# Four sums of weight blocks per combined pair: by adding transfers of GpSimd's queue instead of by VectorE

## The chip, the core and the metric

The kernel runs on one core of one Trainium2 chip. The metric is device time in microseconds (us), the median of several runs; less is better. "ACT" is ScalarE, "DVE" VectorE, "PE" TensorE, "POOL" GpSimd and "SP" SyncE.

## What is computed

One step of a two-layer encoder trunk with 512 prompt rows and 8 x 16 sample rows, 640 rows in all, and a model width of 1024. Each layer does this (the reference, cut to what matters here):

```python
h = x @ w_in            # differential-attention q/k/v | window q/k/v | two branch gates
A = differential attention (8 heads);  B = sliding-window attention (16 heads, sinks)
x = LayerNorm(ALPHA * x + (sigmoid(g_a) * (A @ w_branch_a) + sigmoid(g_b) * (B @ w_branch_b)) @ w_o)
x = LayerNorm(ALPHA * x + relu(x @ w_up) ** 2 @ w_down)
```

All products are fp32-accurate: each operand is split into a high part (fp32r) and the remainder, and each product is three matmuls: high x high, high x low, low x high.

## The kernel before

**Tiling.** Weights stream from DRAM in chunks of 128 x 1024 fp32 (512 KB) through four slots of the tile `w_raw`. SP issues the load of a chunk (L489) once the chunk four places earlier has been split. For each chunk ACT makes the high part by a copy and DVE the low part by a subtraction. Activations are kept transposed, 640 rows in two halves of 320.

**Combined pairs.** Part of the feature tiles are not multiplied one by one. Two tiles (two chunks of weights) form a pair, and each pair's 2 x 2 blocks of weights, a11 and a12 in the first chunk and a21 and a22 in the second, are multiplied with the 2 x 2 blocks of the activations by a scheme with seven block products in place of eight. There are five groups of four pairs in each layer: eight gate tiles (part 0), the branch product of A (`BRANCH`), and parts 1, 2 and 3 of `w_up`. That is 40 pairs in the program. Each block product is 4 x 3 matmuls of 128 x 320, on TensorE in the order o = 0 to 6 (`combined_pair` of the tensor block, L575 to L577).

The stationary operands of the seven products are o=0: a11, o=1: S1 = a21 + a22, o=2: S2 = S1 - a11, o=3: a12, o=4: S3 = a11 - a21, o=5: S4 = a12 - S2, o=6: a22. The four sums are made by DVE in `weight_sums` (L2400, L2403, L2407, L2411). S1 goes to the tile `s_one`; the others overwrite blocks of `w_raw`: S3 takes a21's place, S2 takes a11's, S4 takes a12's. So S2 waits until a11 has been split (`part_ready` 5q+1) and S4 until a12 has been (5q+4); q numbers the pairs through the program.

**Splitting.** For each operand ACT copies the high part (`part_highs`, L1571) and DVE subtracts (`part_low`, L2420). There is one buffer for each o, so the high part for the next pair is made after this pair's product o.

**Seeds.** Three times in each pair ACT copies a partial result from one PSUM bank to another (`up_seed`, L1600): seed 0 after product 0, needed by product 2; seed 1 after product 2, needed by product 4; seed 2 after product 4, needed by product 6. Each engine executes its own instructions in written order. In a pair of `w_up` (parts 1 to 3), ACT's order from one seed to the next is, for pair u:

```python
up_square(u-1, even); up_relu(u-1, odd, half 0); part_highs(u, (6,)); up_seed(u, 0)
up_square_high(u-1, odd); part_highs(u+1, (0,)); up_square(u-1, odd); up_fifth(u)
part_highs(u+1, (1,)); up_seed(u, 1); part_highs(u+1, (2,)); up_relu(u, even, half 0)
part_highs(u+1, (3,)); up_seed(u, 2); up_relu(u, odd, half 1); part_highs(u+1, (4, 5))
up_relu(u, even, half 1); up_square_high(u, even)
```

The gate group and the branch group have the same order without the squares (`gate_pair`, `branch_pair`). DVE, during pair u, makes the lows of the squares of pair u-1 (L2444), the lows of operands 0 to 3 of pair u+1 between the sums, and `up_add` (L2439), which adds `p5` to a bank.

Between the groups stand ordinary row products (`w_down`, L642 to L644) and the attention heads. The first pair of a group is prepared while they run.

Of the kernel before, what the change touches and what calls it, by code (L numbers as in the profile page):

```python
# [26 lines left out]
D = 1024  # L27
# [73 lines left out]
def build(nc, x_rows, x_cols, k_cache, v_cache, swa_kc, swa_vc, swa_k_keep, swa_v_keep, weights, cols,  # L101
# [3 lines left out]
    with ctx:  # L105
# [188 lines left out]
        def up_bank(x):  # L294
            return PS[:, x, 0:HALF]
# [30 lines left out]
        dec_recip, dec_r_ready = sem("dec_recip"), sem("dec_r_ready")  # L326
# [9 lines left out]
        unit_recip, unit_r_ready = sem("unit_recip"), sem("unit_r_ready")  # L336
        unit_second, unit_probs = sem("unit_second"), sem("unit_probs")
# [27 lines left out]
        s_summed, part_hi_made, part_ready = sem("s_summed"), sem("part_hi_made"), sem("part_ready")  # L365
# [120 lines left out]
        def _(sp):  # L486
# [43 lines left out]
            sp.wait_ge(keep_stored, 32)  # L530

# [584 lines left out]
        def _(act):  # L1116
# [426 lines left out]
            def part_highs(l, part, u, products):  # L1543
# [29 lines left out]
            def up_seed(l, part, u, i):  # L1573
# [26 lines left out]
                fn(up_bank(dst), up_bank(src), ACT.Copy).then_inc(seeded, 1)  # L1600
# [174 lines left out]
            for l in range(DEPTH):  # L1775
# [72 lines left out]
                for part in range(FF_PARTS):  # L1848
# [9 lines left out]
                    else:  # L1858
                        q, n = pair_at(l, part, FF_PAIRS - 1)
                        act.wait_ge(part_ready, 5 * (q + 1))  # L1860
                        act.wait_ge(s_summed, 4 * (q + 1))
# [11 lines left out]
        def _(dve):  # L1873
# [86 lines left out]
            def unit_combine(l, h, i):  # L1960
# [59 lines left out]
            def head(l, h, p, first, more, uses):  # L2020
# [18 lines left out]
                v.reciprocal(d_r, d_l).then_inc(dec_recip, 1)  # L2039
                dve.wait_ge(dec_recip, n + 1)  # L2040
                v.tensor_scalar(d_r, d_r, lam_row[:, bass.ds(l, 1)], None, ALU.mult).then_inc(dec_r_ready, 1)
                dve.wait_ge(dec_r_ready, n + 1)
# [47 lines left out]
            def a_sum(l, t):  # L2090
# [14 lines left out]
                elif t == 3:  # L2105
# [3 lines left out]
                    v.tensor_tensor(ta_full[3][:], b22, b12, ALU.subtract).then_inc(t_ready, 1)  # L2109
# [20 lines left out]
            def branch_pair(l, u):  # L2130

                last = u == FF_PAIRS - 1
                if not last:
                    weight_sums(l, BRANCH, u + 1, 1)
                    weight_sums(l, BRANCH, u + 1, 3)
                else:
                    part_low(l, BRANCH, u, 4)
# [5 lines left out]
                else:  # L2143
                    part_low(l, BRANCH, u + 1, 0)
                    weight_sums(l, BRANCH, u + 1, 2)
# [3 lines left out]
                if not last:  # L2149
                    weight_sums(l, BRANCH, u + 1, 4)  # L2150
# [192 lines left out]
            def x_sums(l, which, u):  # L2343
# [20 lines left out]
                elif u == 2:  # L2364
# [4 lines left out]
                    v.tensor_tensor(full[3], b22, b12, ALU.subtract).then_inc(t_ready, 1)  # L2369
# [17 lines left out]

            def weight_sums(l, part, u, which):

                q, n = pair_at(l, part, u)  # L2390
                first, second = raw[:, raw_of(0, n)[0], :], raw[:, raw_of(1, n)[0], :]
                a11, a12, a21, a22 = first[:, 0:BANK], first[:, BANK:D], second[:, 0:BANK], second[:, BANK:D]
                if which == 1:
                    for s in range(2):
                        j, loads = raw_of(s, n)
                        dve.wait_ge(raw_loaded[j], 16 * loads)
                    if q:
                        dve.wait_ge(s_summed, 4 * q - 1)
                        dve.wait_ge(part_ready, 5 * q - 3)
# [436 lines left out]
```

## Time and profile before

| | |
|---|---|
| median of 3 runs | 2199.17 us (2198.41 to 2199.62) |
| the profiled execution's own time | 2201.14 us |
| its span, first to last instruction | 2199.4 us |
| PE busy | 2179.4 us, 99% |
| DVE busy | 1408.5 us, 64% |
| ACT busy | 1135.4 us, 52% |
| POOL busy | 0.2 us |
| mean granted TensorE clock | 0.998 |
| read from and written to HBM | 236.35 and 25.95 MB |

The shares are averages over the whole span. "Idle before" in a row is the time in which the engine stood still ahead of an instruction, and the arrow names what ended it. "Us to landing" of a DMA is the time from the issuing instruction to the semaphore that says that the data has landed.

### The profile page before, as it was taken

The page shows a single profiled execution, that of the slowest core. Times are in us where ns is not written, and L with a number is a line of the kernel's source. Part 1 is how long each engine was busy: PE and PEld are TensorE (multiplying, and loading weights), DVE is VectorE, ACT ScalarE, POOL GpSimd, SP SyncE. Part 2 cuts the span into 40 slices and gives each one's busy share as a digit, 9 for nine tenths or more (in the row PEclk, how much of TensorE's full clock was granted, in tenths as well). Part 3 has the DMA queues.
Part 4 walks back from the last instruction along what each step waited for, and adds up shares of the span by engine and source line. Part 5 has one row for each costly group of instructions (what it writes and reads, how often), then busy time and mean ns, then how long its engine had stood idle before and what let it go on. Part 6 is the DMA issues. An engine that isn't in the chain of part 4 may idle for free.

```text
span 2199.4 us, 38374 instructions
## 1 busy us (share of the span) xinstructions
PE 2179.4 (99%) x15286; PEld 1985.0 (90%) x15290; DVE 1408.5 (64%) x2324; ACT 1135.4 (52%) x2401; POOL 0.2 (0%) x4
## 2 busy tenths in 40 slices
PE   9999999999999999999999999999999999999998
PEld 8988888999989898989889888889999898989897
DVE  6757777766556563736667577776764665736466
ACT  4457766586423353626234676766863232626261
POOL 0000000000000000000000000000000000000000
PEclk9999999999999999999999999999999999999999
DMA  5366562431431222222333765524214312222231
GB/s 185 101 245 247 204 223 84 139 111 59 139 125 39 78 78 85 87 77 87 105 108 105 276 229 193 200 82 144 100 49 149 115 49 77 87 77 87 67 108 75
DMA packets 68160, 268.18 MB, mean 122 GB/s; under 512 B 10984, under 2 KB 12648, under 8 KB 61296
## 3 DMA queue, kind: packets, MB, share of 16 engines
q1 hardware_dynamic: 43136, 152.75, 20.6%
q10 hardware_dynamic: 24848, 112.99, 14.6%
q8 instruction: 122, 2.00, 0.4%
q14 instruction: 54, 0.44, 0.1%
HBM read 236.35 MB, written 25.95 MB: 119 GB/s over the span
## 4 chain that ended last, share of the span: by engine, by line
PE 97%; DVE 2%; issue 1%; ACT 1%; DMA 0%; ACTq 0%; DVEq 0%
PE PS L549 10%; PE PS L643 10%; PE PS L644 10%; PE PS L642 10%; PE PS L551 10%; PE PS L550 10%; PE PS L575 8%; PE PS L576 8%; PE PS L577 8%; PE PS L768 2%; PE PS L793 2%; PE PS L732 1%; PE PS L683 1%; PE PS L898 1%; PE PS L782 1%; PE PS L879 1%
## 5 line engine op out<-in xcount | busy, mean ns | idle before, releaser
L549 PE MATMUL PS<-xt_hi,w_hi 128*128 128x320 f32 x1312 | 421.1, 321 | 4.7 <-ACT rope_c L1271 3.6
L551 PE MATMUL PS<-xt_hi,w_lo 128*128 128x320 f32 x1312 | 405.3, 309 | 0.0
L550 PE MATMUL PS<-xt_lo,w_hi 128*128 128x320 f32 x1312 | 405.1, 309 | 0.0
L1127 ACT ACTIVATE w_hi<-w_raw 128x1024 fp32r<-128x1024 f32 x194 | 203.6, 1058 | 362.4 <-PE PS L644 285.9
L1914 DVE TENSOR_TENSOR w_lo<-w_raw,w_hi 128x1024 fp32r<-128x1024 f32 x194 | 235.4, 1222 | 236.9 <-ACT w_hi L1127 233.3
L642 PE MATMUL PS<-w_hi,act_a_hi 128*128 128x512 f32 x800 | 312.1, 390 | 0.0
L643 PE MATMUL PS<-w_lo,act_a_hi 128*128 128x512 f32 x800 | 311.4, 389 | 0.0
L644 PE MATMUL PS<-w_hi,act_a_lo 128*128 128x512 f32 x800 | 311.4, 389 | 0.0
L549 PEld LDWEIGHTS PS<-xt_hi,w_hi 128*128 128x128 f32 x1312 | 246.6, 188 | 16.3 <-issue 10.1
L550 PEld LDWEIGHTS PS<-xt_lo,w_hi 128*128 128x128 f32 x1312 | 246.9, 188 | 0.1
L551 PEld LDWEIGHTS PS<-xt_hi,w_lo 128*128 128x128 f32 x1312 | 246.3, 188 | 0.0
L644 PEld LDWEIGHTS PS<-w_hi,act_a_lo 128*128 128x128 f32 x800 | 150.2, 188 | 31.3
L642 PEld LDWEIGHTS PS<-w_hi,act_a_hi 128*128 128x128 f32 x800 | 150.2, 188 | 31.0 <-issue 0.5
L643 PEld LDWEIGHTS PS<-w_lo,act_a_hi 128*128 128x128 f32 x800 | 150.2, 188 | 30.5
L1154 ACT ACTIVATE rope_s<-PS 32x320 f32<-32x320 f32 x352 | 150.6, 428 | 50.9 <-DVE z_all L1905 23.2
L2420 DVE TENSOR_TENSOR part_lo<-w_raw,part_hi 128x512 fp32r<-128x512 f32 x130 | 88.7, 689 | 60.7 <-ACT part_hi L1571 58.5
L1571 ACT ACTIVATE part_hi<-w_raw 128x512 fp32r<-128x512 f32 x130 | 80.1, 623 | 33.6 <-DVE w_raw L2407 32.5
L1571 ACT ACTIVATE w_hi<-w_raw 128x512 fp32r<-128x512 f32 x110 | 66.5, 623 | 59.5 <-PE PS L644 48.5
L576 PE MATMUL PS<-t_lo,part_hi 128*128 128x320 f32 x288 | 89.0, 309 | 0.0
L577 PE MATMUL PS<-t_hi,part_lo 128*128 128x320 f32 x288 | 89.0, 309 | 0.0
L575 PE MATMUL PS<-t_hi,part_hi 128*128 128x320 f32 x288 | 89.0, 309 | 0.0
L2257 DVE SCALAR_TENSOR_TENSOR rows<-rows,PS 128x512 f32<-128x512 f32 x100 | 67.2, 685 | 33.9 <-PE PS L644 33.9
(282 smaller groups left out, 4581.3 us busy)
## 6 DMA issues: line engine op xcount, KB each, us to landing
w_raw<-in_weights SPq DMA_DIRECT2D x274, 512.0 KB, 3.5
kc<-in_k_cache ACTq DMA_DIRECT2D x32, 1024.0 KB, 7.7
vc<-in_v_cache ACTq DMA_DIRECT2D x16, 2048.0 KB, 8.8
gates_kept<-a_t ACTq DMA_DIRECT2D x8, 640.0 KB, 6.6
k_out<-k_t ACTq DMA_DIRECT2D x16, 320.0 KB, 2.4
v_out<-rows ACTq DMA_DIRECT2D x2, 2560.0 KB, 17.3
mix_a<-a_t ACTq DMA_DIRECT2D x2, 2560.0 KB, 13.2
rope_c<-gates_kept ACTq DMA_DIRECT2D x10, 320.0 KB, 3.5
```

The lines of the kernel that those rows point to most:

```text
L549: mm(out, wh, hi[:, k, c], start=(k == 0), stop=False)
L550: mm(out, wh, lo[:, k, c], start=False, stop=False)
L551: last = mm(out, wl, hi[:, k, c], start=False, stop=(k == KT - 1))
L575: mm(up_bank(x), wh, moving[0][:, k], start=first and k == 0, stop=False, skip_group_check=True)
L576: mm(up_bank(x), wh, moving[1][:, k], start=False, stop=False, skip_group_check=True)
L577: last = mm(up_bank(x), wl, moving[0][:, k], start=False, stop=(k == KH - 1), skip_group_check=True)
L642: mm(out, xh, wh, start=(k == 0), stop=False)
L643: mm(out, xh, wl, start=False, stop=False)
L644: last = mm(out, xl, wh, start=False, stop=(k == KT - 1))
L1127: fn(w_hi[slot][:], raw[:, j, :], ACT.Copy).then_inc(w_hi_made[s], 1)
L1154: last = fn(rope_s[dst:dst + 32, half * HALF:(half + 1) * HALF], PS[src:src + 32, bank_of(0, half), 0:HALF], ACT.Copy, scale=scale)
L1914: v.tensor_tensor(w_lo[slot][:], raw[:, raw_of(s, n)[0], :], w_hi[slot][:].bitcast(F32), ALU.subtract)\
```

## The change

`weight_sums` and its four calls for each pair are gone. GpSimd, which had no work, gets a program of its own: for each of the 40 pairs five DMAs of 128 x 512 fp32 (256 KB) on its queue, four of which add to what lies at the destination (`accum_op=ALU.add`). All four sums are sums now: S1 = a21 + a22, S2 = a11 + S1, S3 = a11 + a21, S4 = a12 + S2. In order to get the same result, three places take the opposite sign: the third sum of the activations (`b12 - b22`), the first two seeds (scale -1), and the even tile's `up_add` (a subtraction). Two of the operands of the additions are read from DRAM again, where `w_raw` has been overwritten. ACT's waits on `s_summed` become waits on the transfers' semaphores. Some semaphores of the attention part are merged, with the same waits.

```diff
+        @block.gpsimd
+        def _(pool):
+            def pair_sums(l, part, u):
+
+                q, n = pair_at(l, part, u)
+                first, second = raw[:, raw_of(0, n)[0], :], raw[:, raw_of(1, n)[0], :]
+                j, loads = raw_of(1, n)
+                pool.wait_ge(raw_loaded[j], 16 * loads)
+                pool.dma_start(second[:, 0:BANK], weights[2 * n, :, 0:BANK], accum_op=ALU.add)\
+                    .then_inc(s_three_added, 16)
+                if q:
+                    pool.wait_ge(part_ready, 5 * q - 3)
+                if u == 0 and part == 0:
+                    if l == 0:
+                        pool.wait_ge(masks_ready, 2)
+                        pool.wait_ge(lam_link, 6)
+                    else:
+                        pool.wait_ge(input_rows, l * ROW_STEPS)
+                elif u == 0 and part == BRANCH:
+                    pool.wait_ge(unit_pv, 3 * HEADS * (l + 1))
+                elif u == 0 and part == 1:
+                    pool.wait_ge(ln_rows, ROW_STEPS * (l + 1))
+                pool.dma_start(s_one[:], weights[2 * n + 1, :, 0:BANK]).then_inc(s_one_loaded, 16)
+                pool.wait_ge(s_one_loaded, 32 * q + 16)
+                pool.dma_start(s_one[:], weights[2 * n + 1, :, BANK:D], accum_op=ALU.add).then_inc(s_one_loaded, 16)
+                pool.wait_ge(s_one_loaded, 32 * (q + 1))
+                pool.wait_ge(part_ready, 5 * q + 1)
+                pool.dma_start(first[:, 0:BANK], s_one[:], accum_op=ALU.add).then_inc(s_two_added, 16)
+                pool.wait_ge(s_two_added, 16 * (q + 1))
+                pool.wait_ge(part_ready, 5 * q + 4)
+                pool.dma_start(first[:, BANK:D], first[:, 0:BANK], accum_op=ALU.add).then_inc(s_four_added, 16)
...
@@ part_highs @@
-                        act.wait_ge(s_summed, 4 * q + {1: 1, 4: 2, 2: 3, 5: 4}[o])
+                        if o == 1:
+                            act.wait_ge(s_one_loaded, 32 * (q + 1))
+                        elif o == 2:
+                            act.wait_ge(s_two_added, 16 * (q + 1))
+                        elif o == 4:
+                            act.wait_ge(s_three_added, 16 * (q + 1))
+                        else:
+                            act.wait_ge(s_four_added, 16 * (q + 1))
...
@@ up_seed @@
-                fn(up_bank(dst), up_bank(src), ACT.Copy).then_inc(seeded, 1)
+                fn(up_bank(dst), up_bank(src), ACT.Copy, scale=1.0 if i == 2 else -1.0).then_inc(seeded, 1)
...
@@ the third sum of the activations (also for A) @@
-                    v.tensor_tensor(full[3], b22, b12, ALU.subtract).then_inc(t_ready, 1)
+                    v.tensor_tensor(full[3], b12, b22, ALU.subtract).then_inc(t_ready, 1)
...
@@ weight_sums and all its calls @@
-                    v.tensor_tensor(s_one[:], a21, a22, ALU.add).then_inc(s_summed, 1)
-                    v.tensor_tensor(a21, a11, a21, ALU.subtract).then_inc(s_summed, 1)
-                    v.tensor_tensor(a11, s_one[:], a11, ALU.subtract).then_inc(s_summed, 1)
-                    v.tensor_tensor(a12, a12, a11, ALU.subtract).then_inc(s_summed, 1)
...
@@ up_add @@
-                v.tensor_tensor(pair_tile(part, u, odd)[:, HALF:ROWS], up_bank(X2 if odd else X3), p5[:], ALU.add)\
+                v.tensor_tensor(pair_tile(part, u, odd)[:, HALF:ROWS], up_bank(X2 if odd else X3), p5[:],
+                                ALU.add if odd else ALU.subtract)\
                     .then_inc(up_taken, 1)
```

**DVE during a pair of `w_up`, before** (the second pair of part 3 of layer 1; `part_lo` and `w_lo` are low parts, `rope_s` and `rope_c` the odd and the even result tile):

```order
L2400 TENSOR_TENSOR s_one<-w_raw 128x512 [waits s_summed,part_ready,raw_loaded1,raw_loaded0]
L2403 TENSOR_TENSOR w_raw<-w_raw 128x512 [waits s_summed]
L2444 TENSOR_TENSOR act_a_lo<-rope_c,act_a_hi 128x640 [waits pair_sq_done]
L2420 TENSOR_TENSOR w_lo_58<-w_raw,w_hi_56 128x512 [waits w_hi_made1]
L2444 TENSOR_TENSOR act_a_lo<-rope_s,act_a_hi 128x640 [waits pair_sq_done]
L2420 TENSOR_TENSOR part_lo_156<-w_raw,part_hi_155 128x512 [waits part_hi_made]
L2407 TENSOR_TENSOR w_raw<-s_one,w_raw 128x512 [waits part_ready,s_summed]
L2420 TENSOR_TENSOR part_lo_158<-s_one,part_hi_157 128x512 [waits part_hi_made]
L2420 TENSOR_TENSOR part_lo_160<-w_raw,part_hi_159 128x512 [waits part_hi_made]
L2420 TENSOR_TENSOR part_lo_154<-w_raw,part_hi_153 128x512 [waits part_hi_made]
L2439 TENSOR_TENSOR rope_s<-PS,p_152 128x320 [waits chunk_done0,seeded,h_ready,p5_copied]
L2411 TENSOR_TENSOR w_raw<-w_raw 128x512 [waits part_ready,s_summed]
```

The same stretch of DVE, changed:

```order
L2462 TENSOR_TENSOR act_a_lo<-rope_c,act_a_hi 128x640 [waits pair_sq_done]
L2437 TENSOR_TENSOR w_lo_58<-w_raw,w_hi_56 128x512 [waits w_hi_made1]
L2462 TENSOR_TENSOR act_a_lo<-rope_s,act_a_hi 128x640 [waits pair_sq_done]
L2437 TENSOR_TENSOR part_lo_156<-w_raw,part_hi_155 128x512 [waits part_hi_made]
L2437 TENSOR_TENSOR part_lo_158<-s_one,part_hi_157 128x512 [waits part_hi_made]
L2437 TENSOR_TENSOR part_lo_160<-w_raw,part_hi_159 128x512 [waits part_hi_made]
L2437 TENSOR_TENSOR part_lo_154<-w_raw,part_hi_153 128x512 [waits part_hi_made]
L2456 TENSOR_TENSOR rope_s<-PS,p_152 128x320 [waits chunk_done0,seeded,h_ready,p5_copied]
```

The four sums have left DVE; the rest stands in the same order. ACT's instructions stand in the same order as before, with other semaphores in their waits. **GpSimd, changed** (two pairs that follow one another):

```order
L543 DMA w_raw<-in_weights 128x512 [waits raw_loaded3]
L557 DMA s_one<-in_weights 128x512 [waits part_ready]
L559 DMA s_one<-in_weights 128x512 [waits s_one_loaded]
L562 DMA w_raw<-s_one 128x512 [waits part_ready,s_one_loaded]
L565 DMA w_raw<-w_raw 128x512 [waits part_ready,s_two_added]
L543 DMA w_raw<-in_weights 128x512 [waits raw_loaded1]
L557 DMA s_one<-in_weights 128x512 [waits part_ready]
L559 DMA s_one<-in_weights 128x512 [waits s_one_loaded]
```

Before, GpSimd had no DMA. Now each pair's five stand behind the last one of the pair before (L565), which waits until that pair's a12 has been split.

## Rows read from the trace of the kernel before

**Rows 1.** The page: busy time by engine, and the chain that ended last

```profile
PE 2179.4 (99%) x15286; PEld 1985.0 (90%) x15290; DVE 1408.5 (64%) x2324; ACT 1135.4 (52%) x2401; POOL 0.2 (0%) x4
...
PE 97%; DVE 2%; issue 1%; ACT 1%; DMA 0%; ACTq 0%; DVEq 0%
```

**Rows 2.** PE's waits: line <- what ended them: us in total, times, longest

```profile
PE PS L575 <- ACT sv_t L1379: 4.6, 2, 2.3
PE PS L549 <- ACT rope_c L1271: 3.6, 2, 1.8
```

**Rows 3.** Groups of instructions of DVE: the four sums (busy us, mean ns)

```profile
L2407 DVE TENSOR_TENSOR w_raw<-s_one,w_raw 128x512 f32<-128x512 f32 x40 | 27.7, 692 | 4.9 <-DVE part_lo L2420 0.9
L2403 DVE TENSOR_TENSOR w_raw<-w_raw 128x512 f32<-128x512 f32 x40 | 27.7, 692 | 1.4
L2411 DVE TENSOR_TENSOR w_raw<-w_raw 128x512 f32<-128x512 f32 x40 | 27.4, 685 | 1.0
L2400 DVE TENSOR_TENSOR s_one<-w_raw 128x512 f32<-128x512 f32 x40 | 27.3, 683 | 0.0
```

**Rows 4.** Timeline of PE: first matmul of two pairs that follow one another

```profile
2099.98 0.31 PE L575 MATMUL PS<-xt_hi,part_hi 128*128 128x320 f32 x1
...
2112.30 0.31 PE L575 MATMUL PS<-xt_hi,part_hi 128*128 128x320 f32 x1
```

**Rows 5.** Timeline of DVE, pair from 2099.98: lows of operands 0 and 3

```profile
2105.65 0.68 DVE L2420 TENSOR_TENSOR part_lo<-w_raw,part_hi 128x512 fp32r<-128x512 f32 x1
...
2108.67 0.69 DVE L2420 TENSOR_TENSOR part_lo<-w_raw,part_hi 128x512 fp32r<-128x512 f32 x1 [0.15 <-ACT part_hi L1571]
```

**Rows 6.** Timeline of ACT, pairs from 2087.66 and 2099.98: high parts, relu, seeds

```profile
2089.95 0.62 ACT L1571 ACTIVATE part_hi<-w_raw 128x512 fp32r<-128x512 f32 x1
...
2098.11 1.14 ACT L1571 ACTIVATE w_hi<-w_raw 128x512 fp32r<-128x512 f32 x2
2099.89 0.47 ACT L1615 ACTIVATE rope_c<-rope_c 128x320 f32<-128x320 f32 x1 [0.64 <-DVE rope_c L2439]
...
2102.65 0.42 ACT L1600 ACTIVATE PS<-PS 128x320 f32<-128x320 f32 x1
...
2107.16 0.63 ACT L1571 ACTIVATE part_hi<-w_raw 128x512 fp32r<-128x512 f32 x1 [1.12 <-DVE w_raw L2407]
...
2108.98 0.42 ACT L1600 ACTIVATE PS<-PS 128x320 f32<-128x320 f32 x1 [0.34 <-PE PS L577]
```

**Rows 7.** DMA issues: what, queue, count, KB each, median us to landing

```profile
w_raw<-in_weights SPq DMA_DIRECT2D x274, 512.0 KB, 3.5
...
mix_a<-a_t ACTq DMA_DIRECT2D x2, 2560.0 KB, 13.2
...
w_raw<-in_weights SPq DMA_DIRECT2D x2, 256.0 KB, 6.9
...
swk_out<-sk_t ACTq DMA_DIRECT2D x2, 128.0 KB, 2.1
```

**Rows 8.** Windows of one pair each: us, PE, PEld, DVE, ACT, POOL, clock, DMA share, GB/s

```profile
2087.66:2099.98 12.32, 12.32 (x86) 12.31 (x84) 9.07 (x16) 7.01 (x15) 0.00 (x0) 1.00 0.27 85
2099.98:2112.30 12.32, 12.32 (x87) 12.32 (x85) 9.70 (x16) 9.50 (x20) 0.00 (x0) 1.00 0.26 87
```

**Rows 9.** Start of layer 0's branch group: timelines of DVE, ACT, PE

```profile
378.24 0.68 DVE L2420 TENSOR_TENSOR part_lo<-w_raw,part_hi 128x512 fp32r<-128x512 f32 x1
...
379.76 1.15 ACT L1571 ACTIVATE part_hi<-w_raw 128x512 fp32r<-128x512 f32 x2 [2.87 <-DVE w_raw L2407]
...
388.18 0.39 PE L575 MATMUL PS<-aq_hi,part_hi 128*128 128x320 f32 x1 [2.32 <-ACT sv_t L1379]
```

**Rows 10.** Windows of the same place (columns as in rows 8)

```profile
389.60:391.00 1.40, 1.40 (x7) 1.40 (x7) 1.40 (x3) 0.46 (x2) 0.00 (x0) 0.51 0.58 202
391.00:393.00 2.00, 2.00 (x10) 2.00 (x9) 2.00 (x4) 0.50 (x1) 0.00 (x0) 0.50 0.03 8
```

**Rows 11.** Timeline of ACT's queue: one DMA instruction

```profile
386.40 0.35 ACTq L1682 DMA_DIRECT2D rope_c<-gates_kept  x1
```

More of the change, by code:

```diff
@@ L530, in _ @@
             sp.wait_ge(keep_stored, 32)
+        @block.gpsimd
[28 more added lines that the diff above has]
+                pool.dma_start(first[:, BANK:D], first[:, 0:BANK], accum_op=ALU.add).then_inc(s_four_added, 16)
+            for l in range(DEPTH):
+                for part in PAIR_ORDER:
+                    for u in range(FF_PAIRS):
+                        pair_sums(l, part, u)
         @block.tensor
@@ L2038, in head @@
                 dve.wait_ge(dec_exp, 2 * n + 2)
-                v.reciprocal(d_r, d_l).then_inc(dec_recip, 1)
-                dve.wait_ge(dec_recip, n + 1)
+                v.reciprocal(d_r, d_l).then_inc(dec_r_ready, 1)
+                dve.wait_ge(dec_r_ready, 2 * n + 1)
                 v.tensor_scalar(d_r, d_r, lam_row[:, bass.ds(l, 1)], None, ALU.mult).then_inc(dec_r_ready, 1)
-                dve.wait_ge(dec_r_ready, n + 1)
+                dve.wait_ge(dec_r_ready, 2 * n + 2)
                 dve.wait_ge(dec_ot_ready, n)
@@ L2132, in branch_pair @@
                 last = u == FF_PAIRS - 1
[L2133 to L2136, printed above, removed]
+                if last:
                     part_low(l, BRANCH, u, 4)
@@ L2386, in x_sum_low @@
                     .then_inc(t_lo_ready, 1)
[L2388 to L2399, printed above, removed]
-                    v.tensor_tensor(s_one[:], a21, a22, ALU.add).then_inc(s_summed, 1)
-                elif which == 3:
-                    dve.wait_ge(s_summed, 4 * q + 1)
-                    v.tensor_tensor(a21, a11, a21, ALU.subtract).then_inc(s_summed, 1)
-                elif which == 2:
-                    dve.wait_ge(s_summed, 4 * q + 2)
-                    dve.wait_ge(part_ready, 5 * q + 1)
-                    v.tensor_tensor(a11, s_one[:], a11, ALU.subtract).then_inc(s_summed, 1)
-                elif which == 4:
-                    dve.wait_ge(s_summed, 4 * q + 3)
-                    dve.wait_ge(part_ready, 5 * q + 4)
-                    v.tensor_tensor(a12, a12, a11, ALU.subtract).then_inc(s_summed, 1)
             def part_low(l, part, u, o):
@@ L2447, in first_pair_weights @@
             def first_pair_weights(l, part):
-                weight_sums(l, part, 0, 1)
-                weight_sums(l, part, 0, 3)
                 part_low(l, part, 0, 0)
-                weight_sums(l, part, 0, 2)
                 for o in (1, 2, 3):
                     part_low(l, part, 0, o)
-                weight_sums(l, part, 0, 4)
                 part_low(l, part, 0, 4)
@@ L2459, in gate_pair @@
                 last = u == FF_PAIRS - 1
-                if not last:
-                    weight_sums(l, 0, u + 1, 1)
-                    weight_sums(l, 0, u + 1, 3)
-                else:
+                if last:
                     part_low(l, 0, u, 4)
@@ L2488, in combined_pair @@
                 down = nth(l, AT_FF, 4) + part * 8
-                if not last:
-                    weight_sums(l, part, u + 1, 1)
-                    weight_sums(l, part, u + 1, 3)
                 if u > 0:
@@ L2502, in combined_pair @@
                     part_low(l, part, u + 1, 0)
-                    weight_sums(l, part, u + 1, 2)
                     for o in (1, 2, 3):
@@ L2507, in combined_pair @@
                 if not last:
-                    weight_sums(l, part, u + 1, 4)
                     if u + 1 < FF_PAIRS - 1:
```

34 lines of the change are left out of this document (14 added, 20 removed).

## The prediction

> **What bounds the kernel now.** I read the page first: PE is busy for 2179.4 us, 99% of the span, and it makes up 97% of the chain that ended last; DVE is busy for 64% [rows 1]. So DVE's work costs time only where PE waits for it. PE's waits come next: the two largest are 4.6 us in all (2.3 us in each layer, at the start of the branch group) and 3.6 us [rows 2]. No wait of PE for a sum is among them. The windows of single pairs say the same: in both PE is busy for all of 12.32 us, at the full clock, while DVE has 9.07 or 9.70 us of work [rows 8]. The whole that can be won is therefore some 20 us (2199.4 less 2179.4), and hardly any of it hangs on the sums. What counts is whether the sums still come in time. The timelines give this for one pair of `w_up` [rows 4 to 6].
>
> **What is removed.** 4 x 40 sums of about 0.69 us, 110 us of DVE [rows 3]. They lie beside PE's work, so I book 0 us for them, except at the branch start (below). If PE came to wait on DVE's chain, each sum ahead of it would count with 0.6 to 0.7 us.
>
> **What is added.** 200 transfers of 256 KB, five in a pair. Three of them stand on a path to PE one behind the other: S1 in two steps (load, add), then S2. S4 is the fourth. Their traffic, 40 x 5 x 256 KB = 52 MB, doesn't weigh by itself: the DMA engines are busy for 26 or 27% in a pair's window [rows 8]. Their duration does. A sum on DVE takes 0.69 us. For a transfer that adds no row exists. The nearest are the 128 KB store with 2.1 us, a lower bound, the 512 KB load with 3.5, and the 256 KB loads at the start of the program, with much queued beside them, with 6.9, an upper bound [rows 7]. The SBUF to SBUF transfer of 2560 KB takes 13.2 us; above 2.1 us that is 4.3 us for 1 MB, and 256 KB would take 3.2. An adding transfer reads two operands of 256 KB, 512 KB in all, so I take the row of the 512 KB load: **L = 3.5 us** from issue to landing. The DMA engines' page in the Trainium skill (DMA: Bandwidth & Descriptors, Anatomy of one DMA) gives 2.0 us plus bytes / 436e3 for a transfer of GpSimd's queue, so 2.6 us for 256 KB, without an addition; no row here shows one. By it the sum below would come to about 22 us instead of 68.
>
> **The path through ACT in a pair of `w_up`.** ACT works in written order, and the seeds that PE needs stand behind high parts that now wait for transfers. Product o starts 1.76 us x o after the pair (12.32 / 7) [rows 4].
> - Piece 1: from the end of seed 0 (2102.65 + 0.42 = 2103.07) to the end of the low part of operand 0, when the transfer for S2 may go: 2105.65 + 0.68 = 2106.33, so 3.26 us [rows 5, 6]. DVE's sums don't stand ahead of that low part, and it waits for ACT's squares, so their removal doesn't shorten it.
> - Then the transfer, L. Then from the start of the high part of S2 at 2107.16 through relu and the high part of operand 3 to the end of seed 2: 1.90 us without the wait for PE (2108.98 + 0.42 - 2107.16 = 2.24, less 0.34) [rows 6]. PE wants seed 2 four products (7.04 us) after seed 0 let product 2 go. Stall: 3.26 + 3.5 + 1.90 - 7.04 = **1.6 us** at product 6.
> - Piece 2: from the start of the high part of S2 (2107.16) to the end of the low part of operand 3 (2108.67 + 0.69): 2.20 us. Then the transfer for S4, L. Then ACT makes the high part of S4 (two take 1.14 and one 0.62, so 0.52 more), and relu, square, square, relu, high part of a22 and seed 0, from 2099.89 to 2103.07, 3.18 us: 3.70 in all [rows 5, 6].
> - A full turn from seed 0 to seed 0: 3.26 + 3.5 + 2.20 + 3.5 + 3.70 = 16.2 us against 12.32. So each pair in the steady state is 3.9 us longer: 1.6 at product 6 and **2.3** at product 2 of the next pair.
>
> A group of four: in its first pair ACT is free, the high part of the next operand 0 stands at 2089.95 [rows 6], its low part ends at 2089.95 + 0.62 + 0.69 = 2091.3; S2 lands at 2094.8, the low part of operand 3 ends at 2097.0, S4 lands at 2100.5 and seed 0 is done at 2104.2, where product 2 is due at 2099.98 + 3.52 = 2103.5: 0.7, say 0.8 us. Then 1.6, 2.3, 1.6, 2.3. Sum 8.6 us in a group, and six such groups: **52 us**.
>
> **Gate and branch groups.** No squares stand between here, so the turn through ACT is shorter; what binds is GpSimd's own order. The load for S1 is issued behind the transfer for S4 of the pair before: two issues, then load, add and S2 at L each, then 2.20 to the low part of operand 3. An issue of ACT's queue takes 0.35 us [rows 11]; for one of GpSimd's there is no row, and I take 0.4, with 1.3 as the upper bound. Turn: 0.8 + 10.5 + 2.2 = 13.5 against 12.32, 1.2 us in each of two steady pairs, a bit less for the lead at the start: 2 us in a group, 4 groups, **8 us** (up to 6 in a group at 1.3 us).
>
> **The branch start.** ACT has the high part of S2 ahead of the copies that let DVE finish `sk_t` and ACT `sv_t`, for which PE waits 2.32 us. It started at 379.76, after the low part of operand 0 at 378.24 + 0.68 = 378.92 [rows 9]. Without two sums ahead, that low part ends about 1.3 us earlier, at 377.6; plus 3.5 is 381.1, so 1.4 us later than before. Twice: **3 us**.
>
> **The clock.** After that stop of 2.3 us the granted clock stands at 0.51 and 0.50, the lower level of 1.2 GHz [rows 10]; from 389.6 to 393 PE did at half pace what would take half of it, 1.7 us lost. In steady pairs the path through ACT sets the pace and most of the loss hides in the stall; behind the last stall of a group (2.3 us) it doesn't. Not each stall need do it, so I take half of 6 x 1.7: **5 us**.
>
> Sum: 52 + 8 + 3 + 5 = 68 us on the profiled execution's 2201.1, 2269. That execution lies 2 us above the median, so the median becomes 2267; the unknowns lean upwards (contention with the weight loads of SP, 512 KB each, twice in a pair), and I say **2270 us**.
>
> **The rivals.**
> - *Short transfers* (L about 2.6). For: they move half of what the load of 3.5 us moves. Against: 2.1 us is the least for 128 KB. The same formulas give 3.26 + 2.6 + 1.90 - 7.04 = 0.7 and a turn of 14.4, 2.0 a pair, 3.7 us in a group: 22 us and nothing elsewhere, 2221 us. This is what the skill's formula for the duration would bring.
> - *Long transfers* (L of 4.5 to 5). For: a queue of which no row shows a DMA, an addition in the path, five transfers beside two loads; 6.9 us has been seen [rows 7]. Then the turn of `w_up` is 18.2 to 19.2 us, and high parts of S1 hold up seed 1 as well; 16 to 20 us in those groups, 13 to 16 in the others: 150 to 190 us, 2350 to 2390 us.
> - *Hidden anyway.* If an adding transfer took only 2.1 us, the lower bound, stall and turn would be 0.2 and 13.4; less if ACT catches up its relus when DVE's `up_add` no longer stands behind a sum. Some 5 us or less: 2199 to 2204 us.
> - *Faster*, the other side: with transfers of 2.1 us or less, the branch start is won: S2's high part comes earlier by the two sums, and if the stop of 2.3 us falls under what drops the clock, up to 2 x (1.3 + 1.7) = 6 us: 2193 us. It decides below L = 2.2 (377.6 + 2.2 = 379.8, the time of before). No transfer in the rows is that fast save that of 128 KB.
>
> That the sums stay on DVE is excluded by the order of the instructions.
>
> **Numbers.** 0.2% of the time is 4.4 us, about what a measurement can tell from no change. Forecast (L from 3 to 4, 2235 to 2310 us) 0.43; short 0.15; long 0.26; hidden 0.10; faster 0.06. Slower by over 0.2%: 0.43 + 0.15 + 0.26 = 0.84; within: 0.10; faster: 0.06. The range runs from the time of hidden transfers, 2200, to the end of the long ones, 2390.
>
> **What would show it.** Right: transfers of 3 to 4 us to landing; PE idle at L575 of product 2 and of product 6, released by ACT's seeds (L1600 of before), in the last three pairs of each `w_up` group; ACT idle ahead of the high parts of S2 and S4, released by DMA; DVE's busy time down by 110 us; windows of pairs at 16 us instead of 12.32. Wrong: pairs that still take 12.32 us (the transfers are short, or ACT has more slack than I read), or PE waiting for a load of SP, or stalls that begin in a group's first pair at product 4 (L over 4).

## The result and the profile after

The changed kernel takes 2414.41 us in the median (2408.76 to 2415.05, 4 runs) against 2198.79 us before (2198.28 to 2199.62, 4 runs): a ratio of 1.098, 95% interval 1.096 to 1.099, so 216 us slower. The forecast was 2270 us with a range of 2200 to 2390. Its sign was right; the time lies above the range. The profiled execution has a span of 2412.0 us.

The page of after, the lines that answer to [rows 1]:

```profile
PE 2253.0 (93%) x15290; PEld 2041.3 (85%) x15290; DVE 1307.0 (54%) x2164; ACT 1127.1 (47%) x2401; POOL 162.0 (7%) x204
...
q0 software_dynamic: 26240, 52.44, 11.9%
...
PE 68%; DMA 19%; issue 5%; DVE 3%; ACT 3%; POOL 2%; ACTq 0%; DVEq 0%; POOLq 0%
DMA s_one<-in_weights 12%; PE PS L589 9%; PE PS L591 9%; PE PS L590 9%; PE PS L684 7%; PE PS L683 7%; PE PS L682 7%; DMA w_raw<-s_one 5%; PE PS L615 2%; PE PS L616 2%; PE PS L617 2%; PE PS L808 2%; DVE part_lo L2437 2%; PE PS L833 1%; PE PS L772 1%
```

The work went where it was meant to go: DVE is busy for 101.5 us less. But PE is down from 97% to 68% of the chain that ended last, and transfers hold 19% of it, most of that the two steps of S1 (12%) and S2 (5%). PE is also busy for 73.6 us more with the same matmuls, at a mean granted clock of 0.967 instead of 0.998. So of the 212.6 us by which the span grew, PE stands still for 139.0 and works more slowly for 73.6.

The waits of after (line <- what ended them: us, times, longest), to be read beside [rows 2], where no wait of PE had to do with a sum:

```profile
ACT part_hi L1618 <- DMA s_one<-in_weights: 133.6, 34, 7.1
ACT part_hi L1618 <- DMA w_raw<-s_one: 130.0, 40, 6.3
ACT w_hi L1618 <- DMA w_raw<-w_raw: 124.7, 36, 4.9
PE PS L615 <- ACT PS L1647: 116.6, 52, 5.5
PE PS L615 <- ACT sv_t L1419: 8.7, 2, 4.5
```

ACT stands for some 390 us in front of high parts whose sum has not landed, and PE for 116.6 us in front of the seeds (L1647) that ACT has behind them. (Idle time of ACT that PE doesn't wait for costs nothing, so the two don't add up.) The DMA issues (queue, count, KB, median us to landing), to [rows 7]:

```profile
s_one<-in_weights POOLq DMA_DIRECT2D x80, 256.0 KB, 5.2
w_raw<-in_weights POOLq DMA_DIRECT2D x40, 256.0 KB, 5.1
w_raw<-s_one POOLq DMA_DIRECT2D x40, 256.0 KB, 3.3
w_raw<-w_raw POOLq DMA_DIRECT2D x40, 256.0 KB, 3.3
```

S2 and S4, within SBUF, take 3.3 us, close to the L = 3.5 of the forecast. The two steps of S1, from HBM, take 5.1 (the load) and 5.3 (the addition).

Windows of whole groups of four pairs, from the first matmul to the last, that of the branch group to the first matmul behind it (us, PE, PEld, DVE, ACT, POOL, clock, DMA share, GB/s): the gate group, the branch group and one of `w_up`:

```profile
74.85:147.01 72.16, 57.10 (x338) 55.46 (x336) 23.29 (x38) 22.26 (x47) 11.76 (x15) 0.88 0.64 169
410.89:486.11 75.22, 59.28 (x336) 57.52 (x337) 28.02 (x43) 29.30 (x58) 12.96 (x16) 0.86 0.59 156
832.71:900.38 67.67, 56.92 (x337) 55.28 (x336) 25.99 (x40) 34.25 (x68) 10.66 (x13) 0.90 0.52 128
```

Before, gate and `w_up` groups take 49.3 us (four times 12.32) and branch groups, up to the matmul behind them, 51.6 and 51.5. So the six groups of `w_up` lose 18.4 to 21.8 us each, 115 in all, and the four others 22.9 to 25.5 each, 95.5 in all. With 4.1 us more of waiting for `sv_t` that is 214.6 us, where the spans differ by 212.6: within 2 us, the whole loss lies in these groups.

**One turn, step by step.** GpSimd's timeline in the last group of `w_up`, from one S4 (L565) to the next; L543 is S3, L557 and L559 are the two steps of S1, L562 is S2:

```profile
2293.37 0.86 POOL L565 DMA_DIRECT2D w_raw<-w_raw  x1 [5.17 <-DVE part_lo L2437]
2293.90 1.22 POOL L543 DMA_DIRECT2D w_raw<-in_weights  x1
...
2300.14 0.85 POOL L559 DMA_DIRECT2D s_one<-in_weights  x1 [4.45 <-DMA s_one<-in_weights]
...
2305.87 0.86 POOL L562 DMA_DIRECT2D w_raw<-s_one  x1 [4.87 <-DMA s_one<-in_weights]
...
2313.41 0.86 POOL L565 DMA_DIRECT2D w_raw<-w_raw  x1 [6.68 <-DVE part_lo L2437]
```

and ACT's and SyncE's timeline in the same stretch:

```profile
2296.68 0.63 ACT L1618 ACTIVATE w_hi<-w_raw 128x512 fp32r<-128x512 f32 x1 [2.44 <-DMA w_raw<-w_raw]
...
2298.06 3.07 SPq L491 DMA_DIRECT2D w_raw<-in_weights  x2
...
2299.95 0.43 ACT L1647 ACTIVATE PS<-PS 128x320 f32<-128x320 f32 x1
...
2305.61 0.63 ACT L1618 ACTIVATE part_hi<-s_one 128x512 fp32r<-128x512 f32 x1 [3.12 <-DMA s_one<-in_weights]
...
2306.15 0.42 ACT L1647 ACTIVATE PS<-PS 128x320 f32<-128x320 f32 x1
...
2310.65 0.63 ACT L1618 ACTIVATE part_hi<-w_raw 128x512 fp32r<-128x512 f32 x1 [4.08 <-DMA w_raw<-s_one]
```

The turn takes 20.04 us instead of 12.32; it is the longest of the `w_up` groups, whose turns take 16.9 to 20.0. S4 lands after 3.3 us (2293.37 to 2296.68) and seed 0 is done at 2300.38. The low part of operand 0 ends at 2303.63, but S2 can't go: the second step of S1 was issued at 2300.14, behind S4, S3 and its own first step, and lands 5.5 us later. ACT, in its written order, holds seed 1 behind the high part of S1 until 2306.15, so PE stops at product 4 as well. Then S2 takes 4.8 us, 1.5 more than the median (an instruction packet runs beside it, see the last section), and S4 is issued 2.76 us after its landing. The other turns of this group take 18.46 and 16.93 us. PE's stops and what the clock does after them (timeline of PE; a window from 1.3 us after the first):

```profile
2288.17 0.38 PE L615 MATMUL PS<-t_hi,w_hi 128*128 128x320 f32 x1 [2.38 <-ACT PS L1647]
...
2300.52 0.39 PE L615 MATMUL PS<-t_hi,part_hi 128*128 128x320 f32 x1 [1.78 <-ACT PS L1647]
2306.71 0.60 PE L615 MATMUL PS<-t_hi,w_hi 128*128 128x320 f32 x1 [2.44 <-ACT PS L1647]
```

```profile
2289.50:2292.40 2.90, 2.90 (x12) 2.90 (x12) 0.98 (x2) 1.80 (x4) 0.00 (x0) 0.50 0.23 39
```

### The profile page after: what moved, and what is told of

It reads as the page before. It is cut to its first block, busy times and chain, and to the rows that moved or that the text cites. A ratio compares the mean times of both kernels' runs of the same rounds, so it can differ in the third digit from the quotient of the medians.

```text
span 2412.0 us, 38346 instructions
## 1 busy us (share of the span) xinstructions
PE 2253.0 (93%) x15290; PEld 2041.3 (85%) x15290; DVE 1307.0 (54%) x2164; ACT 1127.1 (47%) x2401; POOL 162.0 (7%) x204
## 3 DMA queue, kind: packets, MB, share of 16 engines
q1 hardware_dynamic: 43136, 152.75, 18.4%
## 4 chain that ended last, share of the span: by engine, by line
PE 68%; DMA 19%; issue 5%; DVE 3%; ACT 3%; POOL 2%; ACTq 0%; DVEq 0%; POOLq 0%
DMA s_one<-in_weights 12%; PE PS L589 9%; PE PS L591 9%; PE PS L590 9%; PE PS L684 7%; PE PS L683 7%; PE PS L682 7%; DMA w_raw<-s_one 5%; PE PS L615 2%; PE PS L616 2%; PE PS L617 2%; PE PS L808 2%; DVE part_lo L2437 2%; PE PS L833 1%; PE PS L772 1%
## 5 line engine op out<-in xcount | busy, mean ns | idle before, releaser
L543 POOL DMA_DIRECT2D w_raw<-in_weights x40 | 45.2, 1131 | 1555.8 <-DMA w_raw<-in_weights 1555.8
L615 PE MATMUL PS<-t_hi,part_hi 128*128 128x320 f32 x288 | 98.3, 341 | 47.1 <-ACT PS L1647 46.7
L2437 DVE TENSOR_TENSOR w_lo<-w_raw,w_hi 128x512 fp32r<-128x512 f32 x110 | 74.9, 689 | 109.8 <-ACT w_hi L1618 109.1
L615 PE MATMUL PS<-t_hi,w_hi 128*128 128x320 f32 x224 | 78.9, 352 | 56.6 <-ACT PS L1647 48.3
```

Of the source, the lines that this page charges most:

```text
L615: mm(up_bank(x), wh, moving[0][:, k], start=first and k == 0, stop=False, skip_group_check=True)
L2437: v.tensor_tensor(part_lo[place][:], part_source(n, o), part_hi[place][:].bitcast(F32), ALU.subtract)\
```

## The experiments

Two theories stood at first: that GpSimd's own chain through S1 sets the turn (A), and that the path through ACT behind S2 and S4 does (B). Later the names were "path" (the ring low part of operand 0, S2, low part of operand 3, S4, seed 0 and round again) and "crowding" (the transfers are late since they share the DMA engines with loads that the same event sets free). "C" in the first expectations is that traffic on the DMA engines makes everything slow. All kernels compute the same sums unless it is said.

**S1 by VectorE**

```diff
-                pool.dma_start(s_one[:], weights[2 * n + 1, :, 0:BANK]).then_inc(s_one_loaded, 16)
...
-                pool.dma_start(s_one[:], weights[2 * n + 1, :, BANK:D], accum_op=ALU.add).then_inc(s_one_loaded, 16)
...
+                    v.tensor_tensor(s_one[:], a21, a22, ALU.add).then_inc(s_one_loaded, 1)
```

> S1 is made by VectorE again (one addition a pair, where it stood before the change); S2, S3 and S4 stay transfers. Theory A (GpSimd's own order sets the pace: S4 of one pair, then load and add for S1 of the next at 5.2 us each, then S2 at 3.3 us): two of the four transfers leave the loop, and what is left is the path through ScalarE with S2 and S4 at 3.3 us each, 15.8 us a turn in the groups of w_up and nothing in the gate groups: 6 x 7.4 us plus 10 to 20 for the branch starts and the clock, 2255 to 2265 us. Theory B (the path through ScalarE behind S2 and S4 sets the pace, as forecast, and these transfers are slower than forecast): S1 does not matter much, 2350 us or more. Theory C (the traffic on the DMA engines makes everything slow): 80 of 200 transfers go, time falls by 40% of the 213 us at most, 2330 us.

Measured 2386.97 us, ratio 1.085 (1.083 to 1.088). Only 27 us came back: A alone falls. The issues show what took S1's place (median us to landing):

```profile
w_raw<-in_weights POOLq DMA_DIRECT2D x40, 256.0 KB, 4.7
w_raw<-s_one POOLq DMA_DIRECT2D x40, 256.0 KB, 5.2
w_raw<-w_raw POOLq DMA_DIRECT2D x40, 256.0 KB, 3.3
```

S3 has to wait for S1 here (it overwrites a21). In the first two pairs of each `w_up` group it goes out 0.6 us ahead of S2, and S2 takes 4.9 to 6.6 us; in the gate and branch groups 0.5 to 2.2 us ahead, and S2 takes 3.6 to 8.5. In the last two pairs of a `w_up` group it goes out 5.0 us or more ahead, and S2 takes 3.3 to 4.0 in all but one. Even so the turns that end in those pairs' S4 take 16.8 to 18.1 us, where the path through ACT alone comes to 16.8 (see below). The one whose S2 takes 4.9 us has 18.47 (S4 issued at 2267.45 and 2285.92).

**S1 and S3 from SBUF instead of HBM** (S3 issued after the first step of S1)

```diff
-                pool.dma_start(s_one[:], weights[2 * n + 1, :, 0:BANK]).then_inc(s_one_loaded, 16)
+                pool.dma_start(s_one[:], second[:, 0:BANK]).then_inc(s_one_loaded, 16)
...
+                pool.dma_start(second[:, 0:BANK], first[:, 0:BANK], accum_op=ALU.add).then_inc(s_three_added, 16)
+                pool.dma_start(s_one[:], second[:, BANK:D], accum_op=ALU.add).then_inc(s_one_loaded, 16)
```

> The same five transfers, but those for S1 (copy of a21, addition of a22) and S3 (addition of a11) take their operands from w_raw in SBUF instead of DRAM. If it is the DRAM source that makes them take 5.2 us (theory A), they take 3.3 us like S2 and S4, the loop falls by 3.8 us or more a pair, to about 14, and the time to 2245 to 2270 us. If it is being the first of several on the queue, or a plain cost of GpSimd's queue, they stay near 5 us and the time near 2400 us.

Measured 2455.82 us, 1.117 (1.114 to 1.119), slower still. One turn of its timeline (L556 and L559 are the steps of S1, L558 is S3, L563 S2):

```profile
2310.20 0.86 POOL L556 DMA_DIRECT2D s_one<-w_raw  x1
2314.14 0.87 POOL L558 DMA_DIRECT2D w_raw<-w_raw  x1 [3.07 <-DMA s_one<-w_raw]
...
2314.68 1.20 POOL L559 DMA_DIRECT2D s_one<-w_raw  x1
2314.90 0.93 SPq L491 DMA_DIRECT2D w_raw<-in_weights  x2
...
2323.04 0.86 POOL L563 DMA_DIRECT2D w_raw<-s_one  x1 [7.16 <-DMA s_one<-w_raw]
```

The step that adds for S1 takes 7.9 us here in the median, against 5.3 from HBM, so the source is not the main thing that makes S1 long. S3, the second step of S1 and two loads of 512 KB (issued at 2314.90 and 2315.51) start within 1.4 us, 1.5 MB together, and GpSimd can issue S2 8.4 us after the second step. The source still counts for something: the shortest adding step from HBM takes 4.0 us in the changed kernel (L559) and 3.9 in `loads_held_back`, the shortest addition within SBUF 3.2 (`s4_only`).

**The next pair's S3 and first load of S1 issued before S4**

```diff
+                sum_one_and_two(*pair)
+                if i + 1 < len(pairs) and pair[2] < FF_PAIRS - 1:
+                    sum_one_starts(*pairs[i + 1])
+                sum_four(*pair)
```

> Same transfers and sources; only GpSimd's order changes: within a group, S3 and the first load for S1 of the next pair are issued before GpSimd waits for the low part of a12 and issues S4, instead of behind it. Theory A: about 3 us of waiting (high and low parts of operands 2 and 3) leaves the loop, and S1 of a group's second pair starts up to 6 us sooner; 25 to 35% of the 213 us, 2335 to 2360 us. Theory B: S4 is issued no earlier, so no gain, 2405 us or more. Theory C: no gain.

Measured 2384.87 us, 1.084 (1.082 to 1.087). ACT's wait for S1 fell from 133.6 to 8.7 us, yet only 30 us came back: S4, now behind two transfers, takes 4.5 us instead of 3.3, and S2 3.9.

**S1 and S3 alone, from SBUF; S2 and S4 by VectorE.** The edit is that of the second experiment, with `weight_sums` back on VectorE for S2 and S4.

> S1 and S3 by transfers with SBUF sources, S2 and S4 by VectorE. Nothing of the path behind a low part of the same pair is left to a transfer. S1 can start when the low part of S1 of the pair before is made, some 4.6 us ahead of the pair, and takes 2 x 3.3 us, while ScalarE wants it 5.1 us into the pair. Theory A: no stall in a pair; 2199 us, or 2 to 6 us less if the branch start wins the two sums of VectorE (1.3 us in each layer, and 1.7 us of low clock behind the stop). If pairs still stall, something else than the chain of transfers (contention with VectorE, traffic) is at work.

Measured 2209.76 us, 1.004 (1.003 to 1.006), and no `w_up` group longer than 49.5 us. S1 and S3 have nearly a turn of time where nothing is late. Gate and branch groups lose 1 to 5 us.

**The slot loads held back**

```diff
                 sp.wait_ge(w_ready[before % 2], before // 2 + 1)
+                if before // 2 in next_pair:
+                    sp.wait_ge(s_two_added, 16 * (next_pair[before // 2] + 1))
```

> The changed kernel, with one wait more on SyncE: inside a group the two 512 KB loads that a finished pair sets free start only when S2 of the next pair has landed, so no longer beside S3 and S1. Theory 'crowding' (the transfers are late because the two loads, S3 and S1 are all set free by the same event and share the DMA engines): the loads for S1 land in 3.5 to 4 us instead of 5.1 to 5.3, the pairs of w_up go from 18 to 17 us, the gate and branch groups lose 10 to 15 us instead of 23 to 26; 2335 to 2370 us. Theory 'path' (the chain of sums, high parts and seeds is long whatever else moves): no change, 2400 to 2415 us.

Measured 2402.13 us, 1.092 (1.090 to 1.094). The loads of S1 did become shorter:

```profile
s_one<-in_weights POOLq DMA_DIRECT2D x80, 256.0 KB, 4.2
w_raw<-in_weights POOLq DMA_DIRECT2D x40, 256.0 KB, 4.1
```

so crowding by the slot loads was 0.6 us of S1's first step (5.1 to 4.5) and 1.3 of its second (5.3 to 4.0). But S3 now waits for a load that comes late, and goes out 2.1 to 2.8 us after S4 instead of 0.54; what was won was given back. Of how much crowding costs in the whole this says little.

**S2 and S4 alone; S1 and S3 by VectorE.** GpSimd's program keeps its last six lines.

> S1 and S3 by VectorE, S2 and S4 by adding transfers: nothing of GpSimd's queue comes from HBM. Theory 'path': a turn of w_up is 10.2 us (seed 0 end to S2's issue 3.8, high part of S2 to S4's issue 2.7, high part of S4 to seed 0 end 3.7) plus two transfers of 3.3, so 16.8 against 12.3, about 15 us a group and 90 in six; gate groups 9.8 plus one transfer, 2 to 3 us a group; 2295 to 2310 us. Theory 'crowding': S2 still stands behind the two loads and the gate's 640 KB store and takes 5 to 7 us there, so gate and branch groups lose 8 to 12 each and w_up some 4 more: 2330 to 2350 us.

Measured 2342.51 us, 1.065 (1.062 to 1.067). The second and third turn of a `w_up` group take 16.9 to 18.0 us, the 16.8 of the path and a little more (the first, with its lead, 13.8 to 14.9). The gate groups lose 11.6 and 11.8 us, not 2 to 3. Timelines of ACT's queue, SyncE, GpSimd and ACT there:

```profile
95.49 0.41 ACTq L1671 DMA_DIRECT2D gates_kept<-a_t  x1
...
95.81 2.26 SPq L491 DMA_DIRECT2D w_raw<-in_weights  x2
...
98.95 0.86 POOL L546 DMA_DIRECT2D w_raw<-s_one  x1 [6.95 <-DVE part_lo L2443]
...
104.14 0.63 ACT L1602 ACTIVATE part_hi<-w_raw 128x512 fp32r<-128x512 f32 x1 [5.30 <-DMA w_raw<-s_one]
```

S4's high part lets the gate's 640 KB go to HBM, sets two slots free, and starts the ring's next S2, which then takes 5.2 us. Part of these 5.2 is an instruction packet that runs beside it (see the last section). So the path sets the turns of `w_up`; that crowding makes the loss of the gate groups fits the times and the trace, but was not tried by itself.

**S4 by VectorE, the rest as changed**

```diff
-                pool.dma_start(first[:, BANK:D], first[:, 0:BANK], accum_op=ALU.add).then_inc(s_four_added, 16)
...
+                    v.tensor_tensor(a12, a12, a11, ALU.add).then_inc(s_four_added, 1)
```

> S4 alone by VectorE, S1 to S3 by transfers. Theory 'path': one transfer less in the turn, so w_up at 10.5 + 3.3 to 5 = 14 to 15.5 us a pair, 6 to 11 us a group; S3 and S1 start when S2 has landed, before the slot loads are set free, so the gate groups lose little: 2260 to 2300 us. Theory 'crowding': S1 and S3 now fall beside nothing, S2 beside the loads and takes 5 to 8 us: 2310 to 2340 us.

Measured 2272.40 us, 1.033 (1.031 to 1.034). One transfer of four gives back 142 us: it leaves the ring, and S3 and S1 no longer queue behind it. `w_up` groups lose 4.9 to 7.1 us. The gate groups, which theory "path" expected to lose little, still lose 11.1 and 13.1 us, the branch groups 6.7 and 6.2: the time fell into that theory's range, its account of the gate groups did not hold.

**All sums by VectorE, with the new signs**

> Control: the changed kernel's signs (additions only, the seeds negated) and semaphores, but all four sums by VectorE where they stood before. Both theories: the time of before, 2199 us, within 0.1%. If it is slower, the signs or the merged semaphores of the attention cost something.

Measured 2198.65 us, 0.9995 (0.9985 to 1.0004). Signs and merged semaphores cost nothing. The sums stand where they did before, so this kernel serves as the control.

**S4 alone.** Only the last line of GpSimd's program is left.

> S4 alone by an adding transfer, S1 to S3 by VectorE. Theory 'path, end to end': only the ring from S4 through ACT and back counts. In w_up the turn is 3.7 (high part of S4 to seed 0) + 3.3 (to the low part of operand 0) + 0.8 (S2 on VectorE) + 2.7 + 3.3 = 13.8, so 1.5 us a pair in the steady state, 5 to 6 us a group; in the gate and branch groups 1.8 + 1.4 + 0.8 + 2.7 + 3.3 = 10.0, under 12.3, so nothing; 2230 to 2240 us. Theory 'S4 is the whole loss' (without its transfer the change takes 2272 instead of 2414): 2320 to 2340 us.

Measured 2233.87 us, 1.016 (1.014 to 1.017). Both parts of the path's forecast came in for `w_up` (4.0 to 6.2 us a group) and the gate groups (0.1 and 0.0); the branch groups lose 1.4 and 0.9. GpSimd's timeline in `w_up`, and windows of a `w_up` group and of the gate group:

```profile
2122.36 0.86 POOL L545 DMA_DIRECT2D w_raw<-w_raw  x1 [14.33 <-DVE part_lo L2444]
2136.26 0.86 POOL L545 DMA_DIRECT2D w_raw<-w_raw  x1 [13.05 <-DVE part_lo L2444]
```

```profile
1004.47:1058.35 53.88, 49.99 (x337) 49.27 (x336) 31.63 (x49) 34.26 (x68) 2.58 (x3) 1.00 0.35 103
76.87:126.29 49.42, 49.42 (x337) 49.27 (x336) 27.45 (x44) 23.00 (x47) 2.58 (x3) 1.00 0.56 175
```

A steady turn of 13.9 us against 13.8 worked out, and in the gate group, whose ring of 10.0 us fits into 12.32, nothing.

**S1 and S3 from HBM, S2 and S4 by VectorE**

> S1 and S3 by the change's own transfers from HBM, S2 and S4 by VectorE; with s2_s4_only the other half. Theory 'path': S1 starts as soon as the tile is free and has most of a turn; two loads of 4.5 to 5 us and the issues are 10 to 11 us, under 12.3, so w_up loses 0 to 2 us a group and the others 3 to 6: 2210 to 2235 us, and the two halves add up to less than the whole (143 + 10 to 35 against 215), the rest being S1 pushed back by a late S4. If the halves simply add up: 2265 to 2275 us.

Measured 2224.28 us, 1.012 (1.010 to 1.013). `w_up` loses nothing (49.3 to 49.5 us a group), gate and branch groups 4 to 7. The halves (143 and 25 us) add up to 168, not 216.

**Plain copies instead of additions.** S1 to S4 are no sums here, but copies of one operand; queue, order, bytes and waits stay.

```diff
-                pool.dma_start(first[:, 0:BANK], s_one[:], accum_op=ALU.add).then_inc(s_two_added, 16)
+                pool.dma_start(first[:, 0:BANK], s_one[:]).then_inc(s_two_added, 16)
```

> The changed kernel with all its transfers plain: S1, S2, S3 and S4 are not sums any more but copies of one operand; queue, order, bytes and waits stay. If the addition costs DMA time (a 256 KB addition is on the engines for 1.4 us at 190 GB/s, a plain copy of the same queue for 0.6 us at 430 GB/s): 0.8 us less for each of the two transfers in the turn, 1.6 us x 3 to 4 pairs x 10 groups: 2350 to 2365 us, and S2 and S4 land in 2.5 us. If the time from issue to landing hardly depends on it (the loads of S1 took 5.1 us plain and 5.3 adding): 2400 to 2415 us.

Measured 2314.94 us, 1.053 (1.051 to 1.055), 99 us less than the change. The issues, then packets and q0's share of 16 engines from issue to landing of one S4, first of this kernel (2121.82 to 2124.09), then of `s2_s4_only` with its addition (91.13 to 94.43):

```profile
s_one<-in_weights POOLq DMA_DIRECT2D x80, 256.0 KB, 3.5
w_raw<-in_weights POOLq DMA_DIRECT2D x40, 256.0 KB, 3.3
w_raw<-s_one POOLq DMA_DIRECT2D x40, 256.0 KB, 2.6
w_raw<-w_raw POOLq DMA_DIRECT2D x40, 256.0 KB, 2.3
```

```profile
q0 software_dynamic: 80, 0.26, 30.1%
```

```profile
q0 software_dynamic: 144, 0.26, 46.2%
```

An addition holds the engines for 0.462 x 3.30 = 1.5 us, a plain copy of as many bytes for 0.301 x 2.27 = 0.7, and it lands 0.7 to 1.0 us later within SBUF. S1's first step, plain in both kernels, takes 3.4 us here and 5.1 in the changed kernel, its second 3.8 and 5.3. So an addition also makes its neighbours late: that the plain and the adding step of S1 took about as long as each other in the changed kernel had hidden what an addition costs.

**S1 and S3 of the first branch pair only**, from SBUF, early; all else by VectorE.

```diff
+            for l in range(DEPTH):
+                q, n = pair_at(l, BRANCH, 0)
...
+                pool.dma_start(s_one[:], second[:, 0:BANK]).then_inc(branch_sums, 16)
...
+                pool.dma_start(second[:, 0:BANK], first[:, 0:BANK], accum_op=ALU.add).then_inc(branch_sums, 16)
+                pool.dma_start(s_one[:], second[:, BANK:D], accum_op=ALU.add).then_inc(branch_sums, 16)
```

> All sums by VectorE but two transfers' worth: S1 and S3 of the first pair of each branch group come by transfers within SBUF some 10 us before they are wanted. Theory 'path': those two sums no longer stand ahead of the copies for which PE waits at the start of the branch group (4.6 us in two stops; 2.9 in s1_s3_only), nothing else moves: 2194 to 2198 us. If something else is late there: 2199 us or up to 2 us more.

Measured 2197.81 us, 0.9993 (0.9985 to 1.0002). PE's wait, to [rows 2]:

```profile
PE PS L603 <- ACT sv_t L1407: 2.9, 2, 1.6
```

It fell by 1.7 us, from 4.6 before and 4.7 in the control. The branch groups take 50.1 us each instead of 51.6 and 51.5, but so they do in the control, so that is not the transfers' doing: before, the clock was low behind this stop (0.51, [rows 10]); in the control, behind a stop of 2.37 us in the same place, it is not.

```profile
389.50:391.00 1.50, 1.50 (x12) 1.50 (x12) 1.50 (x3) 0.89 (x2) 0.00 (x0) 1.00 0.62 218
```

So what the transfers win here is 1.7 us, seen in the trace alone; the medians, 2197.81 and the control's 2198.65, don't tell it from nothing. The branch start is the only place where a sum's transfer helped in any run (in `s1_s3_only` and `s1_s3_from_hbm` this wait is 2.9 and 2.5 us).

## Why the prediction was wrong

- **What bounds the kernel, DVE, the branch start**: right. The removed sums bought nothing, and the wait for `sv_t` rose by 4.1 us for a forecast of 3.
- **The path through ACT in `w_up`**: the mechanism was right and a little too short. Between the end of a low part and GpSimd's next issue lie 0.54 us that it left out: `s1_by_dve` has the low part of operand 0 end at 2277.72 and S2 go at 2278.26. With them twice, and 3.3 for each transfer, the ring is 3.26 + 0.54 + 3.3 + 2.74 + 3.3 + 3.68 = 16.8 instead of 16.2; `s2_s4_only` ran at 16.9 to 18.0. Its `w_up` groups lost 13.9 us on average, not 8.6: some 32 us of the miss.
- **L = 3.5 for all five transfers**: the step that failed most. For S2 and S4 it held (3.3). For S1's two steps it was 5.1 and 5.3, and they are issued behind S4 and S3. Of the 5.3, an addition within SBUF is 3.3, the source in HBM some 0.7 (4.0 with the loads held back) and the loads beside it some 1.3. In the turn from 2274.91 the issues follow at 0.53, 0.54, 5.5 and 5.9 us, so S2 goes 12.4 us after S4, where it could have gone after 3.3 + 3.7 + 3.3 + 0.5 = 10.8 through ACT. S1 became the later of the two: 12.4 + 3.3 + 2.8 = 18.5 us a turn, and `w_up` groups lost 18 to 22 us. The forecast took the row of the undisturbed 512 KB load and mentioned contention as a lean. But S3 and S1 go out right behind S4, and SP's loads are set free by the low parts of operands 5 and 6, which wait for the same S4 to land (in the turn shown they end at 2298.03 and 2300.77, the loads go at 2298.06 and 2300.80). A mean DMA share of 27% in a pair's window [rows 8] says nothing on a burst of 1.5 MB.
- **Gate and branch groups, 2 us each**: wrong by more than a factor of ten (22.9 to 25.5). The ring through ACT is indeed short here (`s4_only`: nothing lost in a gate group), but GpSimd's order, for which the forecast had 13.5 us, gives 18.5 by the same addition as above. The gate's own store of 640 KB stands in the same burst, and it was in the profile of before (8 such stores, 6.6 us to landing). The gate groups ran turns of 17.8 to 21.2 us, the branch groups 19.0 to 21.4; why these are longer than 18.5 was not tried.
- **No stall at product 4**: the forecast's sum had stalls at products 2 and 6 alone, and named a stop at product 4 of a group's first pair as a sign of being wrong. That stop is there in all ten groups, 1.9 to 5.1 us long (matmuls counted from each group's first, twelve to a product). In the gate and branch groups PE stops at product 4 of each of the first three pairs, for 3.5 to 5.5 us, and hardly anywhere else; in `w_up` most stops are at product 2, and those at product 6 are 0.2 to 0.8 us where 1.6 was forecast. The second pair of the last group stops at product 4 too, for 2.4 us (shown above).
- **The clock, 5 us**: PE's busy time rose by 73.6 us for the same matmuls, in stretches at the lower clock such as the one shown (0.50). Which stops bring one is left open: at the branch start a stop of 2.3 us did before, one of 2.4 us in the control did not, so the 1.7 us a layer that the rival "faster" counted on were not sure either. But the ring of `s2_s4_only` kept near 16.8 us without any term for it, so inside a group the slow matmuls mostly fill time that PE would have stood. How much of the 216 us is the clock alone was not tried.
- **The rivals**: "long transfers" was the one that came, by its mechanism (high parts of S1 holding seed 1, 16 to 20 us in `w_up` groups); its 13 to 16 for the other groups was too little, and it had 0.26 of the chance. The formula of the Trainium skill (DMA: Bandwidth & Descriptors, Anatomy of one DMA) gives 2.6 us; the plain copies of S2 and S4 took 2.6 and 2.3, so the trace agrees within 0.3 us for a plain copy. A sum within SBUF took 0.7 to 1.0 us more.

What each part costs, from the runs: the ring with S4 alone 35 us; with S2 as well 143; S1 and S3 from HBM alone 25; the remaining 48 are had only together, when S1 starts late behind S4 and the transfers crowd each other. How the 48 split between these two stays open: moving S1 ahead gave 30 us, holding the loads back 12, and each made something else later.

## What to carry to other kernels

Before a sub-microsecond step is moved to a DMA, draw the ring that it stands in, with every wait from one turn to the next, and sum it with a DMA's whole time from issue to landing: a step in the ring costs some 3.3 us here, one outside it nothing until the turn's length is used up. Then list what else the event that starts the transfer sets free, and add the bytes of that burst; the mean DMA share does not show it. Compare a gain with the control too, not only with the kernel before: here the control had 1.5 us of it in each branch group without any transfer. An idle engine's work is worth moving only if somebody waits for it.

## What the runs showed of the hardware

- An adding transfer of 256 KB goes in 144 packets, a plain copy in 80 (16 of either are under 512 bytes, so twice the packets of data), and it lands 0.7 to 1.0 us later than a plain copy within SBUF.
- GpSimd's issues that wait for nothing follow one another at 0.54 us (65 of 70 in the changed kernel, 1.18 at most), though a row is up to 1.3 us long. The first packet of the adding S4 at 91.13 (`s2_s4_only`) leaves 1.4 us after its issue; the plain ones of `plain_copies` leave after 1.1.
- An instruction fetch can hold up a transfer. In `s1_by_dve` S2 is issued at 2278.26; windows of its DMA traffic from 2279.5 to 2281.3 and from 2281.3 to 2283:

```profile
q0 software_dynamic: 135, 0.25, 79.1%
q8 instruction: 1, 0.02, 6.0%
...
q0 software_dynamic: 9, 0.02, 6.9%
```

One packet of the instruction queue takes 6.0% of 16 engines for 1.8 us, 1.7 us of one engine; that engine's nine packets of the sum follow after all the others are done, and ACT starts at 2283.18, 4.9 us after the issue instead of 3.3. That the engine is the same is read from the times. The rest of the record bears it out: in `s4_only`, where GpSimd issues nothing but S4, an instruction packet runs between the first packet and the landing of 8 of the 40, and these take 3.4 to 4.5 us; the 32 others take 3.2 to 3.4, but for one of 3.7. No run changed the instruction packets themselves. Before the change there were 122 of them as well, and PE waited for no transfer.
